# Parameters read as rows and turned by one transpose, strided loads on SyncE's queue, and the state loop begun with the first u tile

## What is computed

```python
h = layer_norm(x, ln_in_g, ln_in_b)
proj = h @ w_in[l]
u, q, k, v, q_idx, k_idx, w_idx, gate_pre = split(proj)
y_ssm = s5_branch(u, lam_re, lam_im, log_dt, b_re, b_im, c_re, c_im, d_skip, w_glu)
y_att = dsa_branch(q, k, v, q_idx, k_idx, w_idx) @ w_attn_proj
g_ssm, g_att = split(sigmoid(gate_pre + b_gate))
h = layer_norm(ALPHA * h + (g_ssm * y_ssm + g_att * y_att) @ w_o, ln1_g, ln1_b)
h = layer_norm(ALPHA * h + moe_ffn(h), ln2_g, ln2_b)
```

## Time and profile before

| | us |
|---|---|
| median of 3 runs | 1899.23 |
| lowest and highest | 1895.12, 1900.89 |
| profiled execution, its own time | 1896.33 |
| its span | 1894.5 |
| busy in the span: PE / DVE / ACT / POOL | 1712.5 / 1550.2 / 1078.5 / 531.7 |
| mean granted clock of TensorE | 0.953 |

### The profile page before, as it was taken

How to read it: one execution, slowest core, us unless ns; L and a number is a source line. 1 busy time by engine, 2 the same in 40 slices (tenths; PEclk the granted TensorE clock), 3 DMA queues, 4 the chain that set the end, 5 groups by cost and what they waited for, 6 DMA issues and landing times.

```text
span 1894.5 us, 22584 instructions
## 1 busy us (share of the span) xinstructions
PE 1712.5 (90%) x7162; PEld 1143.8 (60%) x7162; DVE 1550.2 (82%) x1738; ACT 1078.5 (57%) x1030; POOL 531.7 (28%) x310
## 2 busy tenths in 40 slices
PE   0899887798999768999999999999999999999992
PEld 0433333576666635777777777777777777777761
DVE  1399997794446777999999999999999999999993
ACT  0332321334544525777777777777777777777770
POOL 0165554435206235222222222222222222222220
PEclk9998997899999858999999999999999999999996
DMA  5120111112112366999999999999999999999973
GB/s 151 37 75 14 45 45 45 45 45 89 45 57 78 109 227 258 351 364 359 386 362 364 379 364 361 376 363 361 381 361 359 380 365 356 381 369 362 379 276 103
DMA packets 103796, 465.44 MB, mean 246 GB/s; under 512 B 33184, under 2 KB 33232, under 8 KB 54512
## 3 DMA queue, kind: packets, MB, share of 16 engines
q1 hardware_dynamic: 74064, 441.92, 61.1%
q0 software_dynamic: 9424, 16.86, 3.9%
q10 hardware_dynamic: 20272, 6.23, 1.4%
HBM read 454.81 MB, written 18.92 MB: 250 GB/s over the span
## 4 chain that ended last, share of the span: by engine, by line
PE 72%; DVE 18%; ACT 3%; issue 3%; ACTq 2%; POOL 1%; DMA 1%; DVEq 0%; POOLq 0%
PE ps L1668 19%; PE ps L1670 18%; PE ps L1669 18%; PE ps L1654 2%; PE ps L1419 2%; PE ps L1676 2%; PE ps L1414 2%; DVE scr L1037 1%; DVE scr L1038 1%; DVE scr L1093 1%; DVE top L1092 1%; DVE scr L1035 1%; PE ps L1524 1%; DVE scr L1034 1%; DVE scr L1042 1%
## 5 line engine op out<-in xcount | busy, mean ns | idle before, releaser
L1171 DVE TENSOR_TENSOR w_lo<-raw,w_hi 128x2048 fp32r<-128x2048 f32 x384 | 873.3, 2287 | 81.2 <-ACT w_hi L839 81.2
L839 ACT ACTIVATE w_hi<-raw 128x2048 fp32r<-128x2048 f32 x384 | 736.2, 1918 | 241.8 <-PE ps L1670 241.8
L1668 PE MATMUL ps<-w_hi,x_hi 128*96 128x512 f32 x1024 | 414.8, 405 | 0.0
L1669 PE MATMUL ps<-w_hi,x_lo 128*96 128x512 f32 x1024 | 402.8, 393 | 0.0
L1670 PE MATMUL ps<-w_lo,x_hi 128*96 128x512 f32 x1024 | 402.8, 393 | 0.0
L604 POOL DMA_INDIRECT gate_now<-gate_rows,row_now x32 | 80.2, 2506 | 468.7 <-DVE tok_out L1299 448.2
L1668 PE MATMUL ps<-w_hi,a_hi 128*96 128x512 f32 x512 | 204.2, 399 | 5.7 <-DVE a_lo L1270 5.7
L1670 PEld LDWEIGHTS ps<-w_lo,x_hi 128*96 128x96 f32 x1024 | 166.0, 162 | 70.9
L1668 PEld LDWEIGHTS ps<-w_hi,x_hi 128*96 128x96 f32 x1024 | 168.7, 165 | 65.6 <-issue 0.4
L1669 PEld LDWEIGHTS ps<-w_hi,x_lo 128*96 128x96 f32 x1024 | 166.6, 163 | 63.7
L1670 PE MATMUL ps<-w_lo,a_hi 128*96 128x512 f32 x512 | 202.2, 395 | 0.0
(11 more groups left out here) (296 smaller groups left out, 2335.4 us busy)
## 6 DMA issues: line engine op xcount, KB each, us to landing
raw<-in_w_up SPq DMA_DIRECT2D x256, 1024.0 KB
raw<-in_w_down SPq DMA_DIRECT2D x128, 1024.0 KB
ring<-in_w_in SPq DMA_DIRECT2D x9, 2048.0 KB, 7.8
ring<-in_w_glu SPq DMA_DIRECT2D x4, 1024.0 KB, 6.2
ring<-in_w_o SPq DMA_DIRECT2D x2, 2048.0 KB, 11.9
h<-in_x SPq DMA_DIRECT2D x4, 512.0 KB, 5.6
ring<-in_w_attn_proj SPq DMA_DIRECT2D x1, 2048.0 KB, 9.1
h_rows<-h ACTq DMA_DIRECT2D x4, 512.0 KB
```

The costliest lines, as they stand in the source:

```text
L839: s.activation(hi_of(c)[:, :], raw_of(c), ACT.Copy).then_inc(s_hi, 1)
L1171: d.tensor_tensor(lo_of(c)[:, :], raw_of(c), hi_of(c)[:, :], ALU.subtract).then_inc(s_lo, 1)
L1668: mm(o, xh, hi_of(c)[:, col], start=start, stop=False)
L1669: mm(o, xl, hi_of(c)[:, col], start=False, stop=False)
```

## The change

The small parameters of the front are loaded as rows: `lam_re`, `lam_im`, the LayerNorm gain and bias, `b_gate` and `d_skip` go into one 128-column tile `ptin` (each row 512 contiguous bytes, 84 rows in all), `log_dt` into a two-column tile `ldt`. VectorE spreads `log_dt` over the states, PE transposes the tile once, and ScalarE copies the result from PSUM into `ptab`; `sp_in`, `gbc`, `bgate` and `dskip` become views of it. VectorE waits for the seven loads (`s_ptl`) ahead of its first token tile. The loads of b and c move to SyncE's queue, behind the first weight chunk; the LayerNorm rows, router and router bias go there behind the second. The LayerNorm of a token tile is cut into `measure` and `shift`, and `shift(t - 1)` stands behind `measure(t)`; each tile has its own `mvx` and `rsx`. ScalarE's two Exp stand ahead of its evictions of `hT`. The state loop begins after the first u tile; the other three are put at the head of the list of tiles beside the loop, which then has 20 entries, and `bu(j)` waits for its u tile. The remaining lines of the diff declare semaphores and tiles, and `pe.wait_ge(s_par[3], 64)` ahead of the router becomes 32.

```diff
@@ -399,10 +404,21 @@
                     sp.dma_start(dst.rearrange("p (k n) -> p k n", k=KD), src).then_inc(s_w[n % 2], 16)
 
             chunk(0)
+            for r, nm in enumerate(("b_re", "b_im")):
+                sp.dma_start(braw[:, r], a[nm][0].rearrange("(j w) n c -> (w n) j c", w=2)).then_inc(s_par[1], 16)
+            for r, nm in enumerate(("c_re", "c_im")):
+                src = a[nm][0].rearrange("(q g) c n -> (g c) q n", q=4)
+                for dup in range(2):
+                    sp.dma_start(craw[:, r, :, 64 * dup:64 * dup + 64], src).then_inc(s_par[2], 16)
             sp.dma_start(small[:, :, 0:64], w_in[:, :, C_KI:C_KI + 64]).then_inc(s_small, 16)
             sp.dma_start(small[:, :, 64:136], w_in[:, :, C_KI:C_KI + 72]).then_inc(s_small, 16)
             for n in range(1, NFRONT):
                 chunk(n)
+                if n == 1:
+                    for r, nm in enumerate(("ln_in_g", "ln_in_b")):
+                        sp.dma_start(gb[:, r, :], a[nm].partition_broadcast(P)).then_inc(s_gb1, 16)
+                    sp.dma_start(w_rt[:, :, :], a["w_router"][0].rearrange("(k p) n -> p k n", p=P)).then_inc(s_par[3], 16)
+                    sp.dma_start(b_rt[:, :], a["b_router"][0].partition_broadcast(P)).then_inc(s_par[3], 16)
 
             sp.wait_ge(s_mix, 8)
             for r in range(3):
...
@@ -644,42 +660,30 @@
             s = nc.scalar
             step = Steps(act, s_a)
 
-            act.dma_start(sp_in[:, 0, :], a["lam_re"][0].rearrange("(j w) n -> (w n) j", w=2)).then_inc(s_par[0], 16)
-            act.dma_start(sp_in[:, 1, :], a["lam_im"][0].rearrange("(j w) n -> (w n) j", w=2)).then_inc(s_par[0], 16)
-            for w in range(2):
-                src = a["log_dt"].rearrange("o (j w) -> w o j", w=2)[w].partition_broadcast(STATES)
-                act.dma_start(sp_in[64 * w:64 * w + 64, 2, :], src.rearrange("p o j -> p (o j)")
-                              if len(src.shape) == 3 else src).then_inc(s_par[0], 16)
-            act.dma_start(gbc[:, 0, :], a["ln_in_g"].rearrange("(k p) -> p k", p=P)).then_inc(s_lnp, 16)
-            act.dma_start(gbc[:, 1, :], a["ln_in_b"].rearrange("(k p) -> p k", p=P)).then_inc(s_lnp, 16)
-            for r, nm in enumerate(("b_re", "b_im")):
-                act.dma_start(braw[:, r], a[nm][0].rearrange("(j w) n c -> (w n) j c", w=2)).then_inc(s_par[1], 16)
+            for row, src in ((0, a["lam_re"][0].rearrange("(j w) n -> j (w n)", w=2)),
+                             (SJ, a["lam_im"][0].rearrange("(j w) n -> j (w n)", w=2)),
+                             (R_LN, a["ln_in_g"].rearrange("(k p) -> k p", p=P)),
+                             (R_LN + KD, a["ln_in_b"].rearrange("(k p) -> k p", p=P)),
+                             (R_GATE, a["b_gate"][0].rearrange("(k p) -> k p", p=P)),
+                             (R_SKIP, a["d_skip"][0].rearrange("(q g) c -> q (g c)", q=4))):
+                act.dma_start(ptin[row:row + src.shape[0], :], src).then_inc(s_ptl, 16)
+            act.dma_start(ldt[2 * SJ:3 * SJ, :], a["log_dt"][0].rearrange("(j w) -> j w", w=2)).then_inc(s_ptl, 16)
+            act.wait_ge(s_ptT, 1)
+            s.activation(ptab[:, :], ps[2][:, 0:NPAR], ACT.Copy).then_inc(s_ptab, 1)
 
             for t in range(TT):
                 act.wait_ge(s_var, t + 1)
-                s.activation(rstd[:, 0:1], mv[:, 1:2], ACT.Sqrt, bias=eps[:, 0:1]).then_inc(s_rstd, 1)
-            for r, nm in enumerate(("c_re", "c_im")):
-                src = a[nm][0].rearrange("(q g) c n -> (g c) q n", q=4)
-                for dup in range(2):
-                    act.dma_start(craw[:, r, :, 64 * dup:64 * dup + 64], src).then_inc(s_par[2], 16)
-            act.dma_start(bgate[:, :], a["b_gate"][0].rearrange("(k p) -> p k", p=P)).then_inc(s_par[3], 16)
-            act.dma_start(dskip[:, :], a["d_skip"][0].rearrange("(q g) c -> (g c) q", q=4)).then_inc(s_par[3], 16)
-            for r, nm in enumerate(("ln_in_g", "ln_in_b")):
-                act.dma_start(gb[:, r, :], a[nm].partition_broadcast(P)).then_inc(s_gb1, 16)
-            act.dma_start(w_rt[:, :, :], a["w_router"][0].rearrange("(k p) n -> p k n", p=P)).then_inc(s_par[3], 16)
-            act.dma_start(b_rt[:, :], a["b_router"][0].partition_broadcast(P)).then_inc(s_par[3], 16)
-
-
-            act.wait_ge(s_lnp, 32)
+                s.activation(rsx[:, t, 0:1], mvx[:, t, 1:2], ACT.Sqrt, bias=eps[:, 0:1]).then_inc(s_rstd, 1)
+
+            act.wait_ge(s_ptab, 1)
+            s.activation(spw[:, 0, :], sp_in[:, 2, :], ACT.Exp).then_inc(s_dt, 1)
+            act.wait_ge(s_th, 1)
+            s.activation(spw[:, 2, :], spw[:, 1, :], ACT.Exp).then_inc(s_dt, 1)
             for k in range(KD):
                 act.wait_ge(s_lnT, k + 1)
                 s.activation(hT[:, k, :], ps[4 + k % 4][:, :], ACT.Identity, scale=gbc[:, 0, k:k + 1],
                              bias=gbc[:, 1, k:k + 1]).then_inc(s_hT, 1)
 
-            act.wait_ge(s_par[0], 64)
-            s.activation(spw[:, 0, :], sp_in[:, 2, :], ACT.Exp).then_inc(s_dt, 1)
-            act.wait_ge(s_th, 1)
-            s.activation(spw[:, 2, :], spw[:, 1, :], ACT.Exp).then_inc(s_dt, 1)
             act.wait_ge(s_th, 2)
             s.activation(spw[:, 5, :], spw[:, 4, :], ACT.Sin).then_inc(s_sc, 1)
             step(s.activation(spw[:, 6, :], spw[:, 4, :], ACT.Abs))
...
@@ -734,17 +738,15 @@
                 ins.then_inc(s_tile_a, 1)
 
             n = 0
-            while tiles[n][0] == "u":
-                take(n)
-                n += 1
-                if n == 2:
-                    for q in range(8):
-                        act.wait_ge(s_bbT, q + 1)
-                        r, qq = q // 4, q % 4
-                        s.activation(bT[:, r, qq, :], ps[4 + q % 4][:, 0:P], ACT.Copy).then_inc(s_bT, 1)
-                    act.wait_ge(s_tau, 1)
-                    act.wait_ge(s_const, 2)
-                    phase_products(0)
+            take(n)
+            n += 1
+            act.wait_ge(s_tau, 1)
+            act.wait_ge(s_const, 2)
+            phase_products(0)
+            for q in range(8):
+                act.wait_ge(s_bbT, q + 1)
+                r, qq = q // 4, q % 4
+                s.activation(bT[:, r, qq, :], ps[4 + q % 4][:, 0:P], ACT.Copy).then_inc(s_bT, 1)
             for j in range(SJ):
                 trigs(j)
                 take(n)
...
@@ -955,10 +956,27 @@
                 return d.tensor_scalar(row, row, mv[:, 0:1], rstd[:, 1:2], ALU.subtract, ALU.mult)
 
 
+            def measure(t):
+                dve.wait_ge(s_x[t], 16)
+                for r in range(2):
+                    step(d.bn_stats(stats[:, r, :], h[:, t, 512 * r:512 * r + 512]))
+                d.bn_aggr(mvx[:, t, :], stats[:, :, :]).then_inc(s_var, 1)
+                dve.wait_ge(s_var, t + 1)
+
+            def shift(t):
+                dve.wait_ge(s_rstd, t + 1)
+                step(d.reciprocal(rsx[:, t, 1:2], rsx[:, t, 0:1]))
+                d.tensor_scalar(h[:, t, :], h[:, t, :], mvx[:, t, 0:1], rsx[:, t, 1:2], ALU.subtract, ALU.mult)\
+                    .then_inc(s_xhat, 1)
+
+            dve.wait_ge(s_ptl, 7 * 16)
+            d.tensor_copy(ptin[2 * SJ:3 * SJ, :].rearrange("j (w n) -> j w n", w=2),
+                          ldt[2 * SJ:3 * SJ, :].unsqueeze(2).to_broadcast([SJ, 2, STATES])).then_inc(s_ptx, 1)
             for t in range(TT):
-                dve.wait_ge(s_x[t], 16)
-                norm(h[:, t, :], t + 1, step).then_inc(s_xhat, 1)
-                dve.wait_ge(s_xhat, t + 1)
+                measure(t)
+                if t > 0:
+                    shift(t - 1)
+            shift(TT - 1)
 
             lr, li = sp_in[:, 0, :], sp_in[:, 1, :]
             W = lambda q: spw[:, q, :]
...
@@ -1372,6 +1388,9 @@
             mm, tr = nc.tensor.matmul, nc.tensor.transpose
             pe.wait_ge(s_const, 1)
 
+            pe.wait_ge(s_ptx, 1)
+            tr(ps[2][:, 0:NPAR], ptin[0:NPAR, :], ident[0:NPAR, 0:NPAR]).then_inc(s_ptT, 1)
+
             for k in range(KD):
                 if k >= 4:
                     pe.wait_ge(s_hT, k - 3)
...
@@ -1421,31 +1440,29 @@
 
             arrive(0)
             n = 0
-            for i in range(4):
-                tile(n, 0)
-                n += 1
-                if i == 1:
-
-                    pe.wait_ge(s_par[2], 64)
-                    for r in range(2):
-                        for q in range(4):
-                            tr(ps[2 + r][:, P * q:P * q + P], craw[:, r, q, :], ident[:, :]).then_inc(s_cT, 1)
-
-                    pe.wait_ge(s_bb, 1)
-                    for q in range(8):
-                        r, qq = q // 4, q % 4
-                        if q >= 4:
-                            pe.wait_ge(s_bT, q - 3)
-                        tr(ps[4 + q % 4][:, 0:P], bblk[:, r, 4 * qq:4 * qq + 4, :].rearrange("p j c -> p (j c)"),
-                           ident[:, :])\
-                            .then_inc(s_bbT, 1)
-
-            pe.wait_ge(*taken[n - 1])
```

(46 more changed lines are left out.)

## The result

The changed kernel takes 1868.58 us (median of 4, 1866.42 to 1869.04) against 1900.06 (median of 4, 1895.12 to 1904.45) beside it: ratio 0.9829, 95% interval 0.9811 to 0.9846. That is 31.5 us less; 34.7 were forecast, and the time lies 4.1 us above the predicted one, inside its range. The profiled execution took 1868.76, its span is 1867.0 (before 1894.5).

What follows compares the result with a forecast made beforehand. The front's order bounds the kernel until 97.60 us, then VectorE's state loop to about 319, then PE. 53.4 - 20.6 + 1.9 = 34.7 us gained, set against the median 1899.2: 1864.5 us, 8 in 10 range 1857 to 1880.

Steps and rivals of the forecast that it cites:

- Step 1: Parameter loads leaving ScalarE's front: seven row loads, the last issued at about 4.3 us, all landed at 8.0.
- Steps 2 and 3: Spread, transpose and LayerNorm by measure and shift: last normalised tile ready at 19.6 us instead of 50.58, 31.0 gained.
- Step 4: Between the last normalised tile and the first eviction of hT: 1.0 us instead of 5.5, 4.5 gained.
- Step 5: State loop begun after the first u tile: 8.6 us between them instead of 26.5, 17.9 gained; loop opens at 44.2.
- Step 6: Strided loads of b and c on SP's queue: b lands at 19 to 29 us, c at 24 to 34; free.
- Step 7: Behind the loop, itself again 221.5 us: three v tiles give back 20.6 us; index weights at full clock gain 1.9.
- Later stages move as a block: Stages behind the index weights: everything shifted by 35 us from there.
- Rows late: Rival in the front: rows land at 16.0 us, loop opens at 52.2, time 1872.5; twice that, 1884; chance 17%.
- The tail hidden: Rival behind the loop: something else than PE sets the indexer's start, nothing comes back, 1844 us; chance 4%.
- The strided loads crawl: Rival in the front: b and c land at 91 us, loop opens at about 98, time 1918; chance 5%.
- It does nothing: Rival in the front: another load, chunk 0, sets the first tile, time 1899 us; chance 2%.

Runs made afterwards that it cites:

- rows_behind: Changed kernel, with VectorE's wait for the seven rows behind measure(1) and ScalarE's copy of the transposed rows after its first two Sqrt: 1865.35 us.
- strided_act: Changed kernel, with the six strided loads of b and c issued by ScalarE behind its seven rows instead of by SyncE: 1882.41 us.
- filled: Changed kernel, with the same 20 tiles beside the loop cut into their eight products each, so that no v tile is left behind the loop: 1851.13 us.
- rows_alone: Changed kernel, but with all four u tiles ahead of the state loop again, as in the kernel before: 1868.76 us.
- rows_again: Second run of the changed kernel with all four u tiles ahead of the state loop, beside the changed kernel on one chip: 1868.63 us.
- loop_alone: Kernel before, with only the state loop begun after the first u tile and the other three put beside it: 1909.37 us, ratio 1.0047.
- after_again: The changed kernel itself, unedited, run again as the control on the same chip: 1869.05 us.
- both: Changed kernel, with the tiles beside the loop cut into products and the wait for the seven rows behind measure(1): 1846.42 us.

## Why the prediction was right, and where its terms were off

**Step 1, the rows.** Predicted landed at 8.0, measured 9.3; the bounds were 6.7 and 16.0. In rows_behind the last tile is ready 3.2 us earlier for the 3.4 of measuring that went into this wait.

**Steps 2 and 3, transposing and LayerNorm.** Predicted 11.6 us from the rows to the last normalised tile, measured 10.9 (9.34 to 20.26). The tile costs 2.62, since `shift` and the next `bn_stats` overlap slightly. The 0.4 for a table of the copy's own did not arise: ScalarE loaded that table at 3.81, while it waited.

**Step 4, hT.** Predicted 1.0 from there to the first eviction, measured 0.56. The Exp table load (18.63, 1.28 us) lay beside two shifts. On the drain that the Trainium skill adds (page "ScalarE: Activation LUTs", section "What ACT_TABLE_LOAD costs"), the trace has the table load of the Sin and the op behind it with 0.02 us between them:

```profile
26.85 1.28 ACT L688 ACT_TABLE_LOAD   x1
...
28.15 0.22 ACT L688 ACTIVATE spw<-spw 128x16 f32<-128x16 f32 x1
```

The same step took the evictions and the first u tile at their length before, 15.0 us together; they took 13.2 (20.82 to 34.06). In the kernel before, PE's weight loads for that tile come 0.85 us apart until 66.0 and 0.43 apart behind it; here they are 0.43 to 0.53 apart from the first on.

**Step 5, the opening.** Predicted 44.2, measured 44.77, by another way. The working had b ready at 36.8 and `bu(0)` done at 41, ahead of the trigs at 44.2. The trigs were ready at 43.2; `bu(0)` was not until 44.7. b came at 37.8: its last pair of ops took 1.82 us beside POOL, and 0.87 the time before (34.16), when POOL stood still. `bu(0)` began at 40.93 and took 3.75 us instead of 1.98. The windows of PE's stretch without a matmul and of `bu(0)`, and that of the `bu(0)` of the kernel before:

```profile
35.00:37.80 2.80, 0.00 (x0) 0.00 (x0) 2.66 (x5) 0.87 (x2) 1.70 (x2) 0.91 0.00 0
...
40.90:44.70 3.80, 3.77 (x5) 1.25 (x5) 0.00 (x0) 2.23 (x4) 3.62 (x3) 0.50 0.00 0
```

```profile
94.50:96.40 1.90, 1.89 (x4) 0.66 (x4) 0.00 (x0) 1.90 (x4) 0.57 (x1) 1.00 0.74 193
```

The granted clock was 0.50 here and 1.00 there. In the changed kernel PE waits for b before `bu(0)` and is idle; before, it multiplied u tiles. The prediction had priced work of VectorE and PE at its length in the kernel before. So the stretch from the first u tile to the opening took 10.7 us where 8.6 were counted.

That 52.8 of the 53.4 us came is in part luck: the rows were 1.3 late and this stretch 2.1 too long, the LayerNorm was 0.7, hT 0.4, the evictions and the first tile 1.8 shorter than counted.

**Step 6, the strided loads.** Free, as said: b landed at 15 to 17 us and c at 17 to 19. strided_act shows what they cost where ScalarE issues them.

**Step 7, what comes back.** The three v tiles cost 20.87 us; 20.6 were forecast. filled shows them to be the whole of the give-back: without them the first score follows the loop as closely as before, to 2 us, and these are the index weights' clock. Two terms of this step were off. "It takes its 221.5 us again": 223.7, which is within what executions of one kernel differ by. "**1.9 gained**" at the index weights: their stretch took 8.7 us (291.3 to 299.95) and not 7.6, since the clock fell to a mean of 0.63 in its second half although 20.7 us of matmuls without a gap stood ahead of it. That is 0.8 gained. So 52.8 - 2.2 - 20.9 + 0.8 = 30.5 us are left at the first score, where 34.7 were forecast.

**"Later stages move as a block."** Not quite. The lead of the profiled execution is 30.5 at the first score, 28.9 at the last softmax Exp and 27.5 at the end. Its mean clock is 0.948 against 0.953. Against the medians the gain is 31.5, because the profiled execution of before (1896.33) lay 3.7 below its median. Which stage loses the 3 us was not tried by a run; from the first score to the last Exp rows_alone and rows_again, one kernel, differ by 2.7 us.

**The rivals.** Rows late: partly true, by 1.3 us. The tail hidden: refuted by the third window and by filled. The strided loads crawl: refuted by their landing. It does nothing: chunk 0 did not set the first tile, which began at 26.89, right behind ScalarE's last eviction of hT.

**What the prediction did not say** is that its two halves are worth so unlike sums. It added 17.9 for the early loop and took 20.6 back, and left the reader to see that the difference is negative. loop_alone measures this half at +8.2 us on the kernel before and the pair rows_again and after_again at nothing on the changed one.

## What to carry to other kernels

Work moved out of a serial front into a loop that another engine sets is free only if the loop has slots for it; if each step already has its one tile, the last ones drop out at the end and cost their full price there. Count the slots, and cut the tiles finer before moving them: here that was worth another 18 us, part of it from a shorter loop. And an engine in the path should not issue loads made of thousands of short pieces: six of them, 6,144 pieces in all, held ScalarE for 17.5 us. A loop whose busiest engine has no gap can still be shortened, as the next section shows, where that engine is slowed by a neighbour.

## What the runs showed that was not expected

Cutting the tiles made the loop itself shorter, from 223.0 to 214.7 us between VectorE's first op and its last one's start, with VectorE's busy time down from 216.05 to 205.9 for the same ops. In both (the other kernel with the finer cut) it was 217.9; the ten profiles without the cut lie between 219.6 and 223.5. POOL's ops in it went down too, 127.8 to 116.2 us. The timelines of VectorE and POOL show where VectorE's time goes. Two pieces of one step of the changed kernel:

```profile
207.92 1.27 POOL L500 TENSOR_TENSOR scr<-scr 128x512 f32<-128x512 f32 x1 [5.12 <-ACT scr L698]
208.31 0.69 DVE L1050 TENSOR_TENSOR scr<-ps,scr 128x512 f32<-128x512 f32 x1
...
209.27 1.59 POOL L501 TENSOR_TENSOR scr<-scr 128x512 f32<-128x512 f32 x1
209.77 1.64 DVE L1053 TENSOR_TENSOR scr<-scr 128x512 f32<-128x512 f32 x1
...
216.95 0.69 DVE L1063 TENSOR_TENSOR scr<-scr 128x512 f32<-128x512 f32 x1
```

Counted over the loop of the changed kernel: the 64 `TENSOR_TENSOR` with one input in PSUM (`ps`) take 0.69 us each, beside a POOL op or not (33 are). Of the 128 with both inputs in SBUF, the 64 that run while POOL does nothing take 0.69, the 64 with a POOL op beside them 1.16 on the mean and up to 2.72. Of the 32 scans 6 run alone, in 1.22; the other 26 take 1.69 on the mean and up to 3.25. If all 224 ops ran as they do alone, they would take 171.5 us; they take 213.8 in the changed kernel and 203.6 in filled. So the 10 us of difference lie in ops that have a POOL op beside them: VectorE's loop is 42 us longer for its neighbour in the one, 32 in the other. That the finer slots move ScalarE's takes, and by them POOL's phases against VectorE's ops, is the likely way; no run was made on it, and it stays argued.

The index weights, 64 matmuls of 8 columns, took 9.5, 8.7, 11.6, 10.8 and 9.6 us in before, changed, filled, rows_again and both. Their length follows the clock: the mean granted in them was 0.75, 0.81, 0.61, 0.65 and 0.74, and length times clock is 7.0 to 7.1 us in all five. In the changed kernel 20.7 us of matmuls without a gap, at a granted 1.00, stood ahead of them and did not keep the clock up.

Executions of one kernel differ by up to 13 us. In rows_alone the shortest had the highest mean clock and the longest the lowest (1861.16 at 0.954, 1874.05 at 0.944), but the clock is not all of it: after_again has 1869.05 and 1874.40, both at 0.948. A difference of 7.6 us between two profiled executions was no difference of the medians; the marks up to the first score are steadier than the total.
